# RWKV-7 block inverse: level 6 as 64-column products, level 5's transposed blocks by VectorE

## The reference, cut to what matters

```python
def step(S, inp):
    r_t, w_t, k_t, v_t, a_t, b_t = inp
    sa = jnp.einsum('bhvk,bhk->bhv', S, a_t)
    S = S * w_t[:, :, None, :] + sa[..., None] * b_t[:, :, None, :] + v_t[..., None] * k_t[:, :, None, :]
    return S, jnp.einsum('bhvk,bhk->bhv', S, r_t)
S, ys = lax.scan(step, s0.astype(f32), xs, reverse=reverse)
```

## Time and profile before

| | us |
|---|---|
| median of the three runs | 2361.66 |
| the profiled execution, time | 2364.28 |
| the profiled execution, span | 2362.4 |
| TensorE busy (matmul) | 1809.8 (77%) |
| VectorE busy | 845.7 (36%) |
| ScalarE busy | 505.0 (21%) |
| GpSimd busy | 259.6 (11%) |
| RWKV slots 0 to 19, by time in the span | 800.9 to 1344.8 |

### The profile page before, as it was taken

The page is one execution under the profiler, slowest core; times in us unless marked ns, Lnnn a source line. Parts: engine busy times, 40 slices in busy tenths (PEclk is TensorE's granted clock), DMA queues, the critical chain, the costliest instruction groups (busy, mean ns, idle before and its releaser), DMA issues. The chain is left out here.

```text
span 2362.4 us, 32014 instructions
## 1 busy us (share of the span) xinstructions
PE 1809.8 (77%) x11468; PEld 1276.9 (54%) x11468; DVE 845.7 (36%) x2030; ACT 505.0 (21%) x1146; POOL 259.6 (11%) x480
## 2 busy tenths in 40 slices
PE   5999998799998588888888837653777777777750
PEld 3555755787887577777777614431434434334420
DVE  2000502455554566666666445430111111111114
ACT  2000255233233332333222202110001001001010
POOL 1000002122121322222222000001000000000001
PEclk9999999999999799999999967766988888888975
DMA  9433170000000000000000020008999999999963
GB/s 326 143 107 114 48 267 1 18 1 0 0 0 13 1 1 1 1 6 1 1 1 16 27 102 18 18 9 237 382 383 386 382 384 388 380 385 385 383 230 109
DMA packets 168431, 333.93 MB, mean 141 GB/s; under 512 B 24537, under 2 KB 41177, under 8 KB 168220
## 3 DMA queue, kind: packets, MB, share of 16 engines
q1 hardware_dynamic: 154368, 308.19, 36.1%
q0 software_dynamic: 4720, 14.95, 2.1%
q10 hardware_dynamic: 9264, 9.72, 1.3%
HBM read 303.46 MB, written 29.38 MB: 141 GB/s over the span
## 5 line engine op out<-in xcount | busy, mean ns | idle before, releaser
L997 PE MATMUL ps<-ring,vz 128*64 128x256 f32 x1216 | 164.6, 438 | 52.3 <-DMA ring<-in_expert_up 49.9
L578 PE MATMUL ps<-hT,ring 128*128 128x320 f32 x704 | 195.7, 437 | 8.3 <-ACT hT L1196 5.5
L997 PE MATMUL ps<-fm,vz 128*64 128x256 f32 x1152 | 158.1, 443 | 53.9 <-DMA fm<-in_expert_up 52.8
L578 PEld LDWEIGHTS ps<-hT,ring 128*128 128x128 f32 x704 | 134.4, 192 | 76.1 <-issue 18.2
L1330 ACT COPY ring<-ps 128x256 f32<-128x256 f32 x240 | 89.3, 372 | 360.7 <-PE ps L774 351.8
L774 PE MATMUL ps<-ring 128*128 128x128 f32 x960 | 138.6, 288 | 28.9 <-DVE ring L1703 16.6
L997 PEld LDWEIGHTS ps<-ring,vz 128*64 128x64 f32 x1216 | 100.8, 159 | 110.1 <-issue 68.4
L1977 DVE TENSOR_TENSOR vz<-vz,ps 128x256 f32<-128x256 f32 x37 | 15.6, 421 | 395.9 <-PE ps L997 395.9
L997 PEld LDWEIGHTS ps<-fm,vz 128*64 128x64 f32 x1152 | 96.7, 161 | 109.6 <-issue 77.9
L1703 DVE COPY_PREDICATED ring<-tab,ps 128x256 f32<-128x256 int32 x200 | 84.3, 440 | 191.2 <-PE ps L785 191.0
L774 PEld LDWEIGHTS ps<-ring 128*128 128x128 f32 x960 | 118.2, 193 | 44.1 <-DVE ring L1703 32.0
(11 more groups left out here) (371 smaller groups left out, 2881.8 us busy)
## 6 DMA issues: line engine op xcount, KB each, us to landing
ring<-in_expert_gate SPq DMA_DIRECT2D x19, 2048.0 KB, 19.9
ring<-in_expert_up SPq DMA_DIRECT2D x19, 2048.0 KB, 24.0
hT<-in_expert_down SPq DMA_DIRECT2D x19, 2048.0 KB, 21.5
fm<-in_expert_gate SPq DMA_DIRECT2D x18, 2048.0 KB, 20.2
fm<-in_expert_up SPq DMA_DIRECT2D x18, 2048.0 KB, 24.0
fm<-in_expert_down SPq DMA_DIRECT2D x18, 2048.0 KB, 21.6
x<-in_ada_w SPq DMA_DIRECT2D x8, 2048.0 KB, 10.8
ring<-in_w_in SPq DMA_DIRECT2D x7, 2048.0 KB, 9.2
```

Of the source, the lines that this page charges most:

```text
L578: m = nc.tensor.matmul(ps[2 * (job % 2) + g][:, 0:HALF], ring[:, u, k, P * ct:P * (ct + 1)], hT[:, k, HALF * g:HALF * (g + 1)], start=k == ...
L997: m = nc.tensor.matmul(ps[bank][BT * h:BT * (h + 1), 0:256], e_xT[u][:, k, :], w_[:, k, 256 * h:256 * (h + 1)], start=k == 0, stop=k == KD ...
```

## The change

Level 6: only the blocks of 64 x 64 that change are formed. `last_level_y` and `last_level_xt` issue four products each with 64 stationary and 64 moving columns (contraction over 128); the copies by ScalarE (`copy_last_y`) and VectorE cover 64 partitions and 2 x 64 columns. TensorE signals once after each group of four instead of once for each `d`. `last_level_y` waits for both directions' `r_x` and no longer for level 5's `r_xt`; `last_level_xt` does that.

Level 5: TensorE's transposed products are gone. VectorE copies the new blocks into `r_x` with plain copies on 32 partitions and 2 x 32 columns, two for each `d`, and transposes them into `r_xt` with `transpose` from one partition quarter into another, also two for each `d`.

```diff
             def level_y(it, k):
                     pe.wait_ge(*T.dve.at(f"x{k - 1}{d}_{it}"))
-                    if k == LEVELS - 1:
-                        pe.wait_ge(*T.dve.at(f"xt{k - 1}{d}_{it}"))
...
+            def last_level_y(it):
+                par = it % 2
+                for d in range(2):
+                    pe.wait_ge(*T.dve.at(f"x{LEVELS - 2}{d}_{it}"))
+                for hh in range(2):
+                    for d in range(2):
+                        s_, o, c = 2 * d + hh, RD * (1 - d), RD * d
+                        i = nc.tensor.matmul(ps[d][o:o + RD, RD * hh:RD * (hh + 1)], r_sc[par][:, s_, o:o + RD], r_x[par][:, s_, c:c + RD], start=True, stop=True)
+                i.then_inc(*S.tick(f"y{LEVELS - 1}_{it}"))
+
+            def last_level_xt(it):
+                par = it % 2
+                for d in range(2):
+                    pe.wait_ge(*T.act.at(f"y{LEVELS - 1}{d}_{it}"))
+                    pe.wait_ge(*T.dve.at(f"xt{LEVELS - 2}{d}_{it}"))
+                for hh in range(2):
+                    for d in range(2):
+                        s_, o, c = 2 * d + hh, RD * (1 - d), RD * d
+                        i = nc.tensor.matmul(ps[2 + d][c:c + RD, RD * hh:RD * (hh + 1)], r_y[:, s_, c:c + RD], r_xt[par][:, s_, o:o + RD], start=True, stop=True)
+                i.then_inc(*S.tick(f"xt{LEVELS - 1}_{it}"))
...
             def level_x(it, k):
...
-                    if k >= LEVELS - 2:
-                        for hh in range(2):
-                            s_ = 2 * d + hh
-                            i = nc.tensor.matmul(ps[(2 if k == LEVELS - 1 else 0) + d][:, P * hh:P * (hh + 1)], r_y[:, s_, :], r_xt[par][:, s_, :], start=True, stop=True)
-                        i.then_inc(*S.tick(f"xt{k}{d}_{it}"))
...
                     level_x(it, 5)
-                    level_y(it, 6)
+                    last_level_y(it)
...
-                    level_x(it, 6)
+                    last_level_xt(it)
...
+            def copy_last_y(it):
+                act.wait_ge(*T.pe.at(f"y{LEVELS - 1}_{it}"))
+                for d in range(2):
+                    o, c = RD * (1 - d), RD * d
+                    then(nc.scalar.copy(pair(r_y, d)[o:o + RD, :, c:c + RD], ps[d][o:o + RD, 0:P].rearrange("p (s n) -> p s n", n=RD)), f"y{LEVELS - 1}{d}_{it}")
...
             def level_x(it, k):
...
+                    new = ps[2 + d][:, 0:256].rearrange("p (s n) -> p s n", n=P)
+                    if k < LEVELS - 2:
+                        then(nc.vector.copy_predicated(pair(r_x[par], d), mask_for(d, k), new), f"x{k}{d}_{it}")
+                    else:
+                        for q in range(2):
+                            a, b = 64 * q + 32 * d, 64 * q + 32 * (1 - d)
+                            then(nc.vector.tensor_copy(pair(r_x[par], d)[b:b + 32, :, a:a + 32], new[b:b + 32, :, a:a + 32]), f"x{k}{d}_{it}")
...
             def level_xt(it, k):
...
+                    if k == LEVELS - 1:
+                        dve.wait_ge(*T.pe.at(f"xt{k}_{it}"))
+                        o, c = RD * (1 - d), RD * d
+                        then(nc.vector.tensor_copy(pair(r_xt[par], d)[c:c + RD, :, o:o + RD], ps[2 + d][c:c + RD, 0:P].rearrange("p (s n) -> p s n", n=RD)), f"xt{k}{d}_{it}")
+                    elif k == LEVELS - 2:
+                        dve.wait_ge(*S.at(f"x{k}{d}_{it}"))
+                        for q in range(2):
+                            a, b = 64 * q + 32 * d, 64 * q + 32 * (1 - d)
+                            then(nc.vector.transpose(pair(r_xt[par], d)[a:a + 32, :, b:b + 32], pair(r_x[par], d)[b:b + 32, :, a:a + 32]), f"xt{k}{d}_{it}")
```

More of the change, by code:

```diff
@@ L781, in level_x @@
                     pe.wait_ge(*T.dve.at(f"xt{k - 1}{d}_{it}"))
-                    if k < LEVELS - 1:
-                        for hh in range(2):
-                            s_ = 2 * d + hh
-                            i = nc.tensor.matmul(ps[2 + d][:, P * hh:P * (hh + 1)], r_xt[par][:, s_, :], r_y[:, s_, :], start=True, stop=True)
-                        i.then_inc(*S.tick(f"x{k}{d}_{it}"))
-                    if k >= LEVELS - 2:
-                        for hh in range(2):
-                            s_ = 2 * d + hh
-                            i = nc.tensor.matmul(ps[(2 if k == LEVELS - 1 else 0) + d][:, P * hh:P * (hh + 1)], r_y[:, s_, :], r_xt[par][:, s_, :], start=True, stop=True)
-                        i.then_inc(*S.tick(f"xt{k}{d}_{it}"))
+                    for hh in range(2):
+                        s_ = 2 * d + hh
+                        i = nc.tensor.matmul(ps[2 + d][:, P * hh:P * (hh + 1)], r_xt[par][:, s_, :], r_y[:, s_, :], start=True, stop=True)
+                    i.then_inc(*S.tick(f"x{k}{d}_{it}"))
             def w_pe(it):
```

7 lines of the change are left out of this document (1 added, 6 removed).

## The result

The changed kernel takes 2373.47 us (median of 20 runs, 2365.49 to 2378.82), the kernel before 2362.27 us (20 runs on the same chip): a ratio of **1.0040, with a 95% interval of 1.0030 to 1.0051**. It is still within the 0.5% that the prediction called no change, so the likeliest of the three outcomes was met, but by luck: the sum had the other sign.

What follows compares the result with a forecast made beforehand. The prediction took each slot as a chain passing between TensorE and VectorE, neither full. Slot gains of 11.6 us, 8 lost to the clock and 1.5 regained gave -5.1 us: 2356.6 us, range 2342 to 2371.

Steps and rivals of the forecast that it cites:

- the likeliest of the three outcomes: Whole kernel: time within 0.5% (11.8 us) of the kernel before, chance 0.60; faster had 0.28.
- the sum: Whole kernel: 11.6 us less without the clock, 8 more and 1.5 off for the clock, together -5.1 us.
- The mechanics of the change: Slots without the clock: 0.23 us gained without gates, 0.97 with, 1.3 in slot 19; 11.6 us less.
- VectorE's eight pieces: Level 5's copies and transposes before the second masking: 0.25 us each, 2.0 us for eight, masking 0.11 us later.
- Rival C: Eight instructions between L1703 and the second masking: slower, over 2373.5 us at 0.36 us each, or 0.31 with more falls; chance 0.13.
- rival B: Small VectorE pieces quick (masking 0.7 us earlier, 2338 to 2347 us) or no more clock falls (2348.5 us); chance 0.27.
- Level 6 with 64 columns: From bktm to the next slot: eight products in 0.38 us, 2.10 us instead of 2.44, 0.34 less every slot.
- the switch: TensorE between bktm and level 6's last products: going from 128 to 64 columns charged 0.17 us more.
- the clock's: New thin stretch before bktm: falls in one of two of 11 slots without gates, 1.4 us each, 8 us more.
- 1.5 us off: Clock falls that already exist: cost less where they covered L790, 1.5 us taken off.
- slower: Whole kernel: slower than the kernel before by over 0.5%, chance 0.12.
- supplement of 7 us: Clock falling in nearly every slot without gates: 7 us more, added to 0.31 us VectorE steps in Rival C.

Runs made afterwards that it cites:

- fill_all: Changed kernel plus unread identity products on TensorE in three idle places (before L744, behind level 5, before bktm): 2351.56 us, ratio 0.9941 to the kernel before.
- full_pieces: Changed kernel with level 5's copies and transposes over all 128 partitions, same 64 columns (inverse wrong, timing only): 2357.77 us, ratio 0.9961 to the kernel before.
- the fillers: Changed kernel with unread identity products in one to three of TensorE's thin stretches: ratios 0.9967, 0.9960, 0.9941 and 0.9993 to the kernel before.
- reorder: Changed kernel with level 5's transposes moved behind the second masking and level 6's last products behind akv: 2353.22 us, ratio 0.9944 to the kernel before.
- reorder_fill: reorder plus unread identity products: six behind level 5's first product, three behind its products, three before bktm without gates: 2331.15 us, ratio 0.9851 to the kernel before.

## Why the prediction was wrong, point by point

**The mechanics of the change were right.** Slots at full clock: 26.16 us with gates (the sum had 27.05 - 0.97 = 26.08) and 27.08 without (27.25 - 0.23 = 27.02), read from fill_all, since the changed kernel has none of slots 1 to 18 without gates at PEclk 1.00. Over slots 0 to 18 the gain at full clock is 9.3 us where the sum had 10.3. In slot 19, from level 5's second products to the first product that needs level 6, it is 1352.70 - 1348.63 = 4.07 us, and 1344.83 - 1339.79 = 5.04 before: 0.97 us where the sum had 1.3.

**VectorE's eight pieces were right.** 0.26 us each (0.25 in the sum), chosen by L1748's row against L1778's. full_pieces shows that this was the right reason. Rival C, a price of 0.31 us or more, did not happen, and neither did rival B's quick pieces.

**Level 6 with 64 columns was right.** 0.38 us for the eight products, 0.17 charged for the switch and 0.59 - 0.49 = 0.10 measured behind L753; 2.08 us in all against 2.10. That the total is so close is partly luck: the switch was charged 0.07 too high, and from L759 to the next slot it is 1166.02 - 1164.91 = 1.11 us where the sum kept 1.06.

**The term that failed is the clock's.** The prediction named the mechanism and the place, the thin stretch from L785's four products to bktm, and the price of a fall: 1.4 us. What failed is the step "if one in two of the 11 slots falls there, that is five or six times 1.4: 8 us more". The place and nearly the number were right: seven of the 11 slots fall at bktm, and the kernel before had no fall there. The price was not. The 1.4 us were read from falls at L744 and behind the scans, where TensorE runs 3.4 us at half clock. The new stretches last 6.8 us in six of seven cases, and they lie on bktm, level 6, akv and the next slot's first products, where TensorE itself is the chain; so they cost some 3.0 us each, part of it in the next slot, and 20.7 us together instead of 8. This is also why of slots 1 to 18 sixteen have half-clock time where nine had, slots with gates among them. The "1.5 us off" was nearly so: the falls at the old places, ten before and nine now, cost 14.2 and 13.3 us. Together the clock costs 34.0 - 14.2 = 20 us more where the sum had 6.5, and this difference is the miss: -9.3 + 19.8 = 10.5 us.

**The other side.** The prediction gave "slower" 0.12, by rival C alone, a VectorE price with some clock on top. The case that occurred, right mechanics with falls that cost more than the change gains, was in it only as a supplement of 7 us to another rival. Standing alone, with 20 us for the clock, it would have been -11.6 + 20 = 8 us slower, most of the result.

What stays open: which slots fall, and how long. Slots 10 and 12 have the same thin stretch in front of bktm as slots 4 and 14 and no fall there, slot 9 falls at L744 and slots 11 and 13 do not, and no run here tells why. The changed kernel itself was not run on the chips of the experiments, so the 0.5% to 0.8% of the fillers and of full_pieces rest on ratios from different chips, each known within 0.17%.

## What to carry to other kernels

In a loop that is a chain between engines, work that is taken from TensorE while it waits anyway gains nothing, and can cost more by the clock than the rest of the change gains. Before such a change, find for each slot the thin stretches that it makes or widens, and price the case that all of them fall, as a rival of its own, by the work that stands behind the stretch: where TensorE is the chain, a fall costs more than where it is not. Measure the halves of a change apart: here one half had all the gain and the other most of the risk. Where PEclk is below 1.00 in some slots, first move what the next step of the chain does not need (transposes, outputs, scans) behind what it does; a few products that nobody reads are a cheap test of whether the clock is the cause.

## What the runs showed of the hardware that was not expected

- No wait of TensorE in the rows of waits shown above is over 2.0 us, and the clock falls all the same, where short bursts (0.45 us of level 6's products) stand between such gaps. The Trainium skill, "TensorE: Matmul & The Clock Gate", asks in its closing table that there be no long idle gaps between bursts of matmuls; the trace agrees on the direction, and shows the fall with short waits too.
- Work that computes nothing made a kernel faster: reorder to reorder_fill is 0.9944 to 0.9851, with PEclk from 0.94 to 0.99.
- A VectorE copy on 32 partitions takes as long as one on 128 (221 and 220 ns for 64 columns), and in a row of copies and transposes the narrow ones, which change the quarter each time, are dearer: 2.08 us for eight against 1.25.
- A fall of the clock costs 1.2 to 1.8 us at one place of a slot and some 3.0 (an estimate, above) at another: the half-clock stretches at bktm last 6.8 us and not 3.4, and TensorE is the chain there.
